# Two sets of probabilities, diagonals and softmax columns for the head pairs of a latent attention

## The reference, cut to what matters

```python
def ctx_attention(q, k, v):                       # 256 context queries, context keys
    s = einsum('bqhd,bkhd->bhqk', q, k) * q.shape[-1] ** -0.5
    return einsum('bhqk,bkhd->bqhd', softmax(s), v)

def dense_attention(q_lat, q_ctx, k_lat, v_lat, k_ctx, v_ctx):   # 512 latent queries
    for each block of 128 queries:
        s = concatenate([q_ctx @ k_ctx, q_lat @ k_lat], -1)      # 256 + 512 keys
        p = softmax(s * dk ** -0.5)
        out = p[..., :256] @ v_ctx + p[..., 256:] @ v_lat
```

## Time and profile before

| | |
|---|---|
| median of 3 runs | 4413.17 us (4412.15 to 4413.73) |
| profiled execution, its time / its span | 4408.1 us / 4405.9 us |
| mean granted TensorE clock | 0.955 of full |
| PE busy | 3939.3 us (89% of the span) |
| DVE / ACT / POOL busy | 2149.9 / 1394.3 / 1505.7 us |

### The profile page before, as it was taken

One profiled execution on the slowest core, in us unless ns is written; L12 is line 12 of the kernel. 1 busy time (PEld: TensorE's weight loads), 2 busy tenths in 40 slices (PEclk: granted clock), 3 DMA queues, 4 the chain that ended last, 5 costly groups with the idle time before them and its releaser, 6 DMA issues.

```text
span 4405.9 us, 56655 instructions
## 1 busy us (share of the span) xinstructions
PE 3939.3 (89%) x20925; PEld 3259.6 (74%) x20925; DVE 2149.9 (49%) x3528; ACT 1394.3 (32%) x1862; POOL 1505.7 (34%) x494
## 2 busy tenths in 40 slices
PE   6999979999999979999877777799968889988997
PEld 5888868888888767887755556578748878866885
DVE  6444755446443867554433334676763332234232
ACT  3322334223322333322322232242325432234332
POOL 1443323343444323444200002344436632334341
PEclk9999989999999989999989898899989999999998
DMA  5454423444443423443100001234324421211321
GB/s 182 142 155 150 138 70 131 145 140 145 133 158 109 126 67 122 131 158 91 41 1 10 19 1 58 86 115 152 122 69 133 144 82 54 61 62 57 94 90 55
DMA packets 551756, 440.60 MB, mean 100 GB/s; under 512 B 60332, under 2 KB 549821, under 8 KB 551357
## 3 DMA queue, kind: packets, MB, share of 16 engines
q1 hardware_dynamic: 551613, 438.67, 32.2%
HBM read 431.58 MB, written 2.83 MB: 99 GB/s over the span
## 4 chain that ended last, share of the span: by engine, by line
PE 70%; DVE 13%; issue 8%; ACT 4%; POOL 1%; DMA 1%; SPq 1%; ACTq 0%; DVEq 0%; POOLq 0%
PE ps_all L1813 19%; PE ps_all L1815 18%; PE ps_all L1814 18%; DVE acc L2375 3%; PE ps_all L1561 2%; PE ps_all L1581 1%; PE ps_all L1878 1%; PE ps_all L1566 1%; DMA g_raw<-in_w_mod_dram 1%; PE ps_all L1544 1%; PE ps_all L1663 1%; PE ps_all L1548 1%; DVE full_t L2432 1%; POOL w_lo L789 1%; DVE prod_t L2450 1%
## 5 line engine op out<-in xcount | busy, mean ns | idle before, releaser
L789 POOL TENSOR_TENSOR w_lo<-raw,w_hi 128x2048 fp32r<-128x2048 f32 (+4 forms) x326 | 1343.9, 4123 | 2424.4 <-ACT w_hi L1173 2326.6
L1813 PE MATMUL ps_all<-h_hi,w_hi 128*128 128x512 f32 (+1 forms) x2704 | 1070.1, 396 | 46.8 <-POOL h_lo L795 34.8
L1814 PE MATMUL ps_all<-h_lo,w_hi 128*128 128x512 f32 (+1 forms) x2704 | 1056.6, 391 | 0.0
L1815 PE MATMUL ps_all<-h_hi,w_lo 128*128 128x512 f32 (+1 forms) x2704 | 1056.2, 391 | 0.0
L1173 ACT ACTIVATE w_hi<-raw 128x2048 fp32r<-128x2048 f32 (+4 forms) x320 | 537.8, 1681 | 1593.5 <-PE ps_all L1815 1422.5
L1813 PEld LDWEIGHTS ps_all<-h_hi,w_hi 128*128 128x128 f32 x2704 | 516.2, 191 | 159.6 <-issue 30.3
L2375 DVE SCALAR_TENSOR_TENSOR acc<-g_raw,c_col,acc 128x256 f32<-128x256 f32 x1104 | 618.3, 628 | 1.7
L1815 PEld LDWEIGHTS ps_all<-h_hi,w_lo 128*128 128x128 f32 x2704 | 515.4, 191 | 107.6
L1814 PEld LDWEIGHTS ps_all<-h_lo,w_hi 128*128 128x128 f32 x2704 | 516.1, 191 | 102.4 <-issue 1.0
L1813 PE MATMUL ps_all<-hid_hi,w_hi 128*128 128x512 f32 (+1 forms) x1272 | 480.7, 378 | 27.2 <-DVE hid_lo L2453 17.5
L1815 PE MATMUL ps_all<-hid_hi,w_lo 128*128 128x512 f32 (+1 forms) x1272 | 472.5, 371 | 0.0
(11 more groups left out here) (335 smaller groups left out, 5186.3 us busy)
## 6 DMA issues: line engine op xcount, KB each, us to landing
raw<-in_w_ffn_gu_dram SPq DMA_DIRECT2D x88, 1024.0 KB, 5.0
g_raw<-in_w_mod_dram SPq DMA_DIRECT2D x72, 1024.0 KB, 5.0
raw<-in_ffn_w_in_dram SPq DMA_DIRECT2D x66, 1024.0 KB, 5.0
g_raw<-in_ada_w_dram SPq DMA_DIRECT2D x48, 1024.0 KB, 5.3
raw<-in_w_ffn_down_dram SPq DMA_DIRECT2D x32, 768.0 KB, 4.8
raw<-in_w_ffn_down_dram SPq DMA_DIRECT2D x32, 640.0 KB, 4.3
raw<-in_ffn_w_out_dram SPq DMA_DIRECT2D x24, 768.0 KB, 4.9
raw<-in_ffn_w_out_dram SPq DMA_DIRECT2D x24, 640.0 KB, 4.4
```

The source lines that it names most:

```text
L789: nc.gpsimd.tensor_tensor(v(w_lo), v(raw), v(w_hi).bitcast(F32), ALU.subtract).then_inc(sem["w_split_lo"], 1)
L1813: nc.tensor.matmul(o, whi, mhi, start=first, stop=False)
L1814: nc.tensor.matmul(o, whi, mlo, start=False, stop=False)
L1815: return nc.tensor.matmul(o, wlo, mhi, start=False, stop=last)
```

## The change

`prob` and `diag` become two sets, even and odd pairs, and the `stat` columns become four for each head and parity. `prob_odd` lies in the second half of `g_raw`, the diagonals move to byte 6144 of it. The waits reach back two pairs in place of one. The order of the instructions on every engine, their number and their shapes stay as they are.

```diff
-    diag = sb("diag", [P, 2, P], at=g_raw_at + 9216)
+    diag = sb("diag", [P, 2, 2, P], at=g_raw_at + 6144)
     prob_t = sb("prob_t", [P, 2, T], at=spare)
-    prob = sb("prob", [P, 2, T], at=spare + 6144)
+    prob = (sb("prob_even", [P, 2, T], at=spare + 6144), sb("prob_odd", [P, 2, T], at=g_raw_at + 8192))
...
         def exps(n, g):
             hp, ctx, q = MLA_PAIRS[n]
             act.wait_ge(sem["s_max"], base_of("s_max", U) + 2 * n + g + 1)
-            if n >= 1:
-
-                act.wait_ge(sem["turned0"], base_of("turned0", U) + 2 * n + g - 1)
-                if not MLA_PAIRS[n - 1][1]:
-                    act.wait_ge(sem["turned1"], base_of("turned1", LU) + MLA_LAT[n - 1] + g + 1)
+            if n >= 2:
+
+                act.wait_ge(sem["turned0"], base_of("turned0", U) + 2 * n + g - 3)
+                if not MLA_PAIRS[n - 2][1]:
+                    act.wait_ge(sem["turned1"], base_of("turned1", LU) + MLA_LAT[n - 2] + g + 1)
+            at = 8 * (n % 2) + 4 * g
...
-            nc.scalar.activation(prob[:, g, 0:W], pair[:, C:C + W], ACT.Exp, scale=DQ ** -0.5,
-                                 bias=stat[:, 4 * g + 1:4 * g + 2], accum_out=stat[:, 4 * g + 2:4 * g + 3]).then_inc(sem["s_exp"], 1)
+            nc.scalar.activation(prob[n % 2][:, g, 0:W], pair[:, C:C + W], ACT.Exp, scale=DQ ** -0.5,
+                                 bias=stat[:, at + 1:at + 2], accum_out=stat[:, at + 2:at + 3]).then_inc(sem["s_exp"], 1)
...
-                ins = nc.tensor.matmul(ps_all[:, 4, t * P:(t + 1) * P], prob[:, g, t * P:(t + 1) * P], diag[:, g, :], start=True, stop=True)
+                ins = nc.tensor.matmul(ps_all[:, 4, t * P:(t + 1) * P], prob[n % 2][:, g, t * P:(t + 1) * P], diag[:, n % 2, g, :], start=True, stop=True)
...
-            s_ = lambda t: stat[:, 4 * g + t:4 * g + t + 1]
-            if n >= 1:
-
-                dve.wait_ge(sem["s_shared"], base_of("s_shared", U) + 2 * n + g - 1)
+            s_ = lambda t: stat[:, 8 * (n % 2) + 4 * g + t:8 * (n % 2) + 4 * g + t + 1]
+            if n >= 2:
+
+                dve.wait_ge(sem["s_shared"], base_of("s_shared", U) + 2 * n + g - 3)
...
-            share(dve, ch, lambda t: stat[:, 4 * g + t:4 * g + t + 1], base_of("s_exp", U) + 2 * n + g + 1, diag[:, g, :])
+            share(dve, ch, lambda t: stat[:, 8 * (n % 2) + 4 * g + t:8 * (n % 2) + 4 * g + t + 1], base_of("s_exp", U) + 2 * n + g + 1, diag[:, n % 2, g, :])
```

More of the change, by code:

```diff
@@ L1565, in turn @@
                 for t in range(3, 6):
-                    ins = nc.tensor.matmul(ps_all[:, 5, (t - 3) * P:(t - 2) * P], prob[:, g, t * P:(t + 1) * P], diag[:, g, :], start=True, stop=True)
+                    ins = nc.tensor.matmul(ps_all[:, 5, (t - 3) * P:(t - 2) * P], prob[n % 2][:, g, t * P:(t + 1) * P], diag[:, n % 2, g, :], start=True, stop=True)
                 ins.then_inc(sem["turned1"], 1)
```

## The result

The changed kernel takes 4304.9 us (median of 4 runs, 4301.5 to 4306.2) against 4413.5 us (4 runs), a ratio of 0.9752 with a 95% interval of 0.9735 to 0.9769: 108.6 us less. The forecast was 95 us less, 4318 us. The profiled execution took 4306.24 us, 102 us less than the profiled one before.

What follows compares the result with a forecast made beforehand. It took the latent attention to be bound by PE and ACT waiting on each other (turn, exps, copy, turn, exps, scores), PE idle about 124 us. Savings of 88 + 7 = 95 us from 4413.2 gave 4318 us, range 4297 to 4340.

Steps and rivals of the forecast that it cites:

- the likeliest case: Latent attention step: PE becomes the bound and the clock pattern is kept; 4318 us, chance 0.71.
- The chain: Latent pairs: turn, exps, copy, turn, exps, scores set the cycle; it falls from 10.26 to 7.5 us.
- The start of the exponential: Latent pairs: exps(n+1, 0) waits only for its maximum, starting 1.18 us after the reduction starts.
- the signs named beforehand: Profile after: latent cycles 7.5 us, PE idle before line 1561 under 0.2, step some 95 shorter, same busy sum.
- Free by cover: Attention step: the `s_shared` wait, buffer places in `g_raw` and ACT's bank reads beside DVE's reductions cost nothing.
- The wait was never the last one: Attention pairs: exps and copy stand in one order on ACT anyway, so no change; 4413 us, chance 0.04.
- the copy takes the place of the wait: Some 24 cycles: exps(n+1, 0) is held until both reductions are done, 22 us given back; 4340 us, chance 0.09.
- the clock stays down: Latent pairs: PE work doubles at the lower clock; if all 24 long ones went slow, 4488 us, chance 0.03.
- The sum: Whole attention step: 88 us over four iterations plus 7 us from the clock, 95 us saved.
- The second case: Denser loop keeps its clock: mid-loop slow stretches vanish, a further 15 us come back; 4303 us, chance 0.13.
- the clock term: Slow stretches come about as often, end somewhat sooner, give 7 us: 5 after context pairs, 2 at iteration starts.
- the full-clock terms: Pairs of the attention step at full clock: 21.9 us saved per iteration, 88 us over four.

Runs made afterwards that it cites:

- experiment 1: The changed kernel with its doubled buffers, but exps waits again for the turn of the pair just before: 4415.3 us, ratio 1.0012 against the kernel before.
- experiment 3: The changed kernel, but the second head's exps waits again for the turn one pair back, only the first goes ahead: 4366.7 us, ratio 0.9906.
- experiment 4: The changed kernel, but the first head's exps waits again for the turn one pair back, only the second goes ahead: 4358.2 us, ratio 0.9896.
- experiment 2: The changed kernel with two sets for `prob` only, one for `diag` and `stat`: 4312.2 us, ratio 0.9785 against the kernel before.
- experiment 5: The kernel before, with 7 and 5 idle matmuls in PE's two gaps behind the turns of n = 5: 4397.4 us against 4415.3, ratio 0.9954.
- experiment 7: The changed kernel, with four of six value tiles computed behind an iteration's first scores and their ACT copies moved later: 4285.5 us, ratio 0.9709.
- experiment 8: The kernel before, with 3 and 2 idle matmuls behind the two turns of n = 6: 4426.6 us against 4415.8, ratio 1.0022.
- experiment 6: The changed kernel, with 7 idle matmuls in the one gap left at n = 5: 4307.8 us, ratio 0.9760 against the kernel before.

## Why the prediction was right, and where it was off

The first half of the likeliest case held: PE became the bound of the pairs, and the time lay in the range. The second half, that the clock keeps its pattern, did not. By its own steps:

| pair | forecast, now and then | measured, now and then (full clock) |
|---|---|---|
| latent, next latent | 10.26, 7.5 | 10.26, 7.63 |
| latent, next context | 7.69, 5.8 | 7.69, 5.91 |
| context, next context | 5.99, 4.6 | 5.99, 4.69 |
| context, next latent | 7.61, 6.6 | 7.61, 6.48 |
| latent after context | 9.39, 7.2 | 9.39, 7.30 |

- **The chain.** That exps(n+1, 0), the copy and exps(n+1, 1) were the chain, and the wait its only cause, is shown by experiments 1, 3 and 4: waits back, gain gone; each head alone gives 46 and 55 us, in cycles as computed. The 0.1 us by which the latent cycle is longer than forecast lie behind the second half of turn(n, 1). It starts 6.76 us behind the scores, where 6.75 was computed, and the next scores follow 0.87 us later in place of 0.75.
- **The start of the exponential** 1.18 us behind the reduction was 1.26 (2208.56 - 2207.30), and the copies are what PE just waits for, as named. Of the signs named beforehand one failed: PE's busy sum did not stay the same but fell from 410 to 387 us, because less of the work ran at the lower clock.
- **Free by cover.** The diagonals and columns: more than free, not needed (experiment 2).
- **The rivals.** "The wait was never the last one" and "the copy takes the place of the wait" fall with the cycle of 7.63 us; "the clock stays down" with the clock of 0.95.
- **The sum.** Taken pair by pair from the starts of the scores, the 109 us of the step divide into 44.5 in the latent pairs n = 1, 2, 7 and 8, 14.7 in n = 3 and 9, 5.4 in n = 4, 5.8 in n = 5, 22.8 in n = 6, 8.7 in the first pairs and 7.4 behind the last scores. The forecast had 44, 15, 6, 4, 14 (9 and the 5 of the clock), 8 and 4.

The term that was mis-sized is the clock: "I take it that the slow stretches come about as often, end somewhat sooner, and give 7 us: 5 there". Of the 14 us that the forecast of the step lacks, 9 are at n = 6, and most of the rest is at n = 5 and behind the last scores, parts of which were slow before. At n = 6 the full-clock part of the saving is 8.5 us (9.39 to 7.30 in three iterations, 9.55 to 7.30 in the fourth, where 9.55 is that of experiment 5). So the clock gave 14 us there, where the forecast had 5. The slow pair came twice in place of three times, and cost 1.6 us each (8.94 against 7.30) in place of 5.8. The windows view, first three rows of the kernel before within its first slow pair, then the kernel after around the first of its two:

```profile
2246.00:2248.00 2.00, 2.00 (x10) 0.75 (x6) 0.00 (x0) 0.00 (x0) 0.00 (x0) 0.50 0.00 0
2252.00:2254.00 2.00, 2.00 (x10) 2.00 (x11) 1.08 (x3) 0.00 (x0) 0.00 (x0) 0.50 0.00 0
2256.00:2258.00 2.00, 1.68 (x8) 1.71 (x9) 0.29 (x1) 0.17 (x1) 0.00 (x0) 0.50 0.00 0
...
2236.00:2238.00 2.00, 1.89 (x8) 1.08 (x9) 0.45 (x2) 0.86 (x3) 0.00 (x0) 0.65 0.04 8
2238.00:2240.00 2.00, 2.00 (x8) 0.84 (x6) 0.00 (x0) 0.00 (x0) 0.00 (x0) 0.50 0.00 0
2240.00:2242.00 2.00, 2.00 (x18) 1.04 (x15) 0.71 (x1) 0.00 (x0) 0.00 (x0) 0.99 0.00 0
```

The clock fell as the next scores began (2236.55) and was back some 3.5 us later, while the kernel before stayed down through 8 us of a busy PE (2246 to 2254, with the earlier trace rows) and nearly to the end of the pair. The second case, a loop that keeps its clock, had 4303 us, and the result lies nearer to that number: 9 of the 15 us that it adds came back at n = 6. But the case itself did not occur in that form, for slow pairs are left. The size of the clock term was assumed and not worked out; the time lay in the range because the full-clock terms, 88 of the 95 us, came out as the table shows. By the rule of the Trainium skill ("TensorE: Matmul & The Clock Gate", "Part 1: The HAM clock gate"), activity releases the throttle. Experiment 5 (gaps filled, no fall) and experiment 7 (0.99) go with it. Experiment 8, with 10 us at 0.50 and PE busy throughout, is against a prompt release. Why a slow stretch of the changed kernel ends so much sooner stays open: filling the gaps within it (experiment 8) was not shown to do it.

The forecast was worked against the profiled execution, whose step shrank by 109 us and whose total by 102. The medians differ by 108.6. Differences of 5 to 10 us between executions lie outside the step.

## What to carry to other kernels

When a wait of one engine shows up beside a large idle total, follow it until the bounding engine waits for it; here that gave each cycle to 0.13 us before anything was built, by the durations of the rows and one row of a place where the operation waited for nothing else. Double only the buffer whose reader is on the chain: `prob` alone brought the whole gain. After that, look at the bounding engine's remaining idle time for work whose inputs are ready and for a bank that is free; moving four tiles of values there gave 19 us more, about half of it (12 of 24 us of the step) by keeping the clock up.

## What was not expected of the hardware

- 48 matmuls that compute nothing made the kernel before 18 us faster, because the lower clock after the gaps cost more than they do (the pair behind them took 15.2 to 15.4 us in three iterations of four before, and 9.4 to 9.6 us with them).
- A slow stretch, once begun, is not ended at once by a busy PE: 10 us at 0.50 with PE busy throughout in experiment 8, 8 us in the kernel before, some 3.5 us in the changed kernel.
- Slow stretches move. Filling one gap (experiments 5 and 6) removed them there, and slow stretches at the ends or starts of iterations were longer in the one profiled execution of each, by 1 to 3 us, so that a gain of a few us from the clock is not to be counted on in one place.
